# A two-layer encoder with a mixture of experts: the router works by pairs of token tiles, and the first expert's rows come from one-hot products

## What is computed

```python
def hier_moe(h, w_group, b_group, w_er, b_er, w_gate, w_up, w_down):
    ...
    g_sel = jnp.argmax(g_logit, axis=-1)             # one of 4 groups
    ...
    top_v, top_i = lax.top_k(e_logit, MOE_TOP_K)     # two of its 8 experts
    gate = jax.nn.softmax(top_v, axis=-1) * p_g[:, None]
    ...
    def expert_block(args):
        xb, e = args
        return (jax.nn.silu(xb @ w_gate[e]) * (xb @ w_up[e])) @ w_down[e]
```

## Time and profile before

| | |
|---|---|
| median of 3 runs | 1590.0 us (1588.47 to 1594.48) |
| profiled execution | 1584.55 us |
| span in its profile | 1582.7 us |
| PE busy | 1388.3 us (88%) |
| DVE busy | 529.7 us (33%) |
| moved by DMA | 479.23 MB |

### The profile page before, as it was taken

One profiled execution on the slowest core, in us unless ns is written; L12 is line 12 of the kernel. 1 busy time (PEld: TensorE's weight loads), 2 busy tenths in 40 slices (PEclk: granted clock), 3 DMA queues, 4 the chain that ended last, 5 costly groups with the idle time before them and its releaser, 6 DMA issues. The chain is left out here.

```text
span 1582.7 us, 18640 instructions
## 1 busy us (share of the span) xinstructions
PE 1388.3 (88%) x6901; PEld 640.5 (40%) x6901; DVE 529.7 (33%) x1248; ACT 244.0 (15%) x522; POOL 194.4 (12%) x362
## 2 busy tenths in 40 slices
PE   7999999999988888887889978899997887888786
PEld 4544574553333332332334456455332332333232
DVE  6999985251110111111141159335111111011115
ACT  3211121120000000000020047212100000000002
POOL 5200000011111111111000000001121111111100
PEclk9999999999999999999999989999999999999999
DMA  8314436279999999999995100537999999999996
GB/s 251 119 58 94 56 121 266 93 287 385 402 426 427 427 426 427 426 427 426 427 367 194 54 1 2 213 123 302 369 419 427 426 426 426 428 426 428 425 429 257
DMA packets 74021, 479.23 MB, mean 303 GB/s; under 512 B 16152, under 2 KB 23064, under 8 KB 49392
## 3 DMA queue, kind: packets, MB, share of 16 engines
q1 hardware_dynamic: 61392, 454.36, 71.1%
q0 software_dynamic: 11152, 19.27, 3.4%
q10 hardware_dynamic: 1424, 4.89, 0.8%
HBM read 468.01 MB, written 26.74 MB: 313 GB/s over the span
## 5 line engine op out<-in xcount | busy, mean ns | idle before, releaser
L700 PE MATMUL psum<-ring,work 128*64 128x512 f32 x992 | 475.1, 635 | 89.2 <-DMA ring<-in_moe_w_up 89.2
L701 PE MATMUL psum<-ring,work 128*64 128x512 f32 x992 | 475.7, 636 | 0.0
L700 PEld LDWEIGHTS psum<-ring,work 128*64 128x64 f32 x992 | 140.1, 146 | 397.5 <-issue 310.5
L713 PE MATMUL psum<-ring,work 128*64 128x512 f32 x992 | 226.5, 598 | 40.1 <-DVE work L886 39.8
L883 DVE TENSOR_TENSOR work<-work,psum 64x512 f32<-64x512 f32 x64 | 44.2, 690 | 557.4 <-ACT work L840 557.3
L840 ACT ACTIVATE work<-psum 64x512 f32<-64x512 f32 x64 | 37.8, 590 | 800.0 <-PE psum L701 800.0
L701 PEld LDWEIGHTS psum<-ring,work 128*64 128x64 f32 x992 | 140.2, 146 | 2.0
L713 PEld LDWEIGHTS psum<-ring,work 128*64 128x64 f32 x992 | 67.3, 136 | 157.5 <-issue 132.6
L889 DVE COPY work<-psum 128x512 f32<-128x512 f32 x60 | 41.4, 691 | 231.5 <-PE psum L713 231.5
L1793 PE MATMUL psum<-ring,hT 128*128 128x512 f32 x256 | 113.5, 600 | 0.0
L1086 POOL DMA_INDIRECT work<-h_dram,ints x64 | 66.8, 1043 | 56.9 <-POOL ints L1079 53.1
(11 more groups left out here) (382 smaller groups left out, 1406.9 us busy)
## 6 DMA issues: line engine op xcount, KB each, us to landing
ring<-in_moe_w_gate SPq DMA_DIRECT2D x62, 2048.0 KB, 16.9
ring<-in_moe_w_up SPq DMA_DIRECT2D x62, 2048.0 KB, 21.5
ring<-in_moe_w_down SPq DMA_DIRECT2D x62, 2048.0 KB, 21.9
ring<-in_hyb_w_in SPq DMA_DIRECT2D x5, 2048.0 KB, 8.9
work<-y_dram SPq DMA_DIRECT2D x8, 1024.0 KB, 9.4
ring<-in_swa_w_qkv SPq DMA_DIRECT2D x3, 2048.0 KB, 17.8
x_sb<-in_x SPq DMA_DIRECT2D x8, 512.0 KB, 6.3
y_dram<-x_sb SPq DMA_DIRECT2D x1, 4096.0 KB, 18.5
```

Source lines behind the costliest of these rows:

```text
L700: nc.tensor.matmul(bank[2 + b][0:BLK, :], x, g[:, c, :], start=c == 0, stop=c == KC - 1)
L701: i = nc.tensor.matmul(bank[2 + b][BLK:P, :], x, u[:, c, :], start=c == 0, stop=c == KC - 1)
L713: i = nc.tensor.matmul(bank[6 + b][BLK * hf:BLK * (hf + 1), :], HTE[b][:, c, :], d[:, c, hf * HALF:(hf + 1) * HALF], start=c == 0, stop=c ...
```

## The change

The router works on tiles 0 and 1 first and on tiles 2 and 3 later, each pair with logits in a bank of its own (7 and 4), a chain `groups(b)`, `experts(b)`, `places(b)` and counts of its own. The logits of tile 2 are computed as soon as its halves are out of PSUM. ACT copies both halves of the last tile; DVE evacuates a tile ahead of norming the next, and ACT takes the root behind its copy. The gather of the first expert's rows, its 4 transposes and their copy are gone. In their place DVE makes for each tile a one-hot of 64 columns (`OH0`), and `pe_x_first` multiplies `hN` by it: 16 matmuls of 64 columns for each pair. ACT copies the first pair's result (`XF`) and DVE adds the second's. The lists serve from the second expert on, and the products for target rows stand behind the first expert's gate and up products (`pe_targets`). The fillers shrink: before there are, in columns, 2 x 512 ahead of the logits of tile 2, 256 ahead of the last logits, 7 x 512 behind them, 2 x 512 and 256 behind the counts, and 3 x 512, 256 and 512 around `pe_x` of the first expert; what is left is 256 ahead of the last logits, 2 x 512 behind the first count and 256 behind the last. The load to `W2[2]` now waits for the logits only; that to `W2[1]`, which lies over `hN`, waits for the last product that reads `hN` and stands behind it.

```diff
+        def act_norm_evac_last(act, A_, n):
+
+            act.wait_ge(n_hp.s, 8 * n + 2 * NT)
+            A_(nc.scalar.copy(hT[:, 4:8, (NT - 1) * P:NT * P],
+                              bank[norm_bank(n, NT - 1) + 1][:, :].rearrange("p (c n) -> p c n", c=4)), n_ea)
...
+        OH0 = cut(WK, 9216, NT * BLK)
+        PL2 = cut(WK, 9472, 8 * BLK)
+        XF = XT[0].rearrange("p c (g n) -> p c g n", g=2)
+
+        AS = [rt("AS")[:, 3 * NE * b:3 * NE * (b + 1)] for b in range(2)]
...
-            pe.wait_ge(n_ea.s, NT * (2 * l + 1) + t + 1)
-            pe.wait_ge(n_ed.s, NT * (2 * l + 1) + t + 1)
+            pe.wait_ge(n_ea.s, act_evacs(2 * l + 1, t))
             if t == 0:
                 pe.wait_ge(g_wr.s, l + 1)
             wr = rt("wr").rearrange("p (c n) -> p c n", c=KC)
             for c in range(KC):
-                i = nc.tensor.matmul(bank[7][:, 36 * t:36 * t + 36], hT[:, c, t * P:(t + 1) * P], wr[:, c, :],
+                if c == KC // 2 and t < NT - 1:
+                    pe.wait_ge(n_ed.s, dve_evacs(2 * l + 1, t))
+                elif c == KC // 2:
+                    pe.wait_ge(n_ea.s, act_evacs(2 * l + 1, t) + 1)
+                i = nc.tensor.matmul(bank[LGB[t // 2]][:, 36 * (t % 2):36 * (t % 2) + 36], hT[:, c, t * P:(t + 1) * P], wr[:, c, :],
                                      start=c == 0, stop=c == KC - 1)
-            if t == NT - 1:
+            if t % 2:
                 i.then_inc(g_lg.s, 1)
 
+        def pe_x_first(pe, b, done):
+
+            for c in range(KC):
+                for t in range(2 * b, 2 * b + 2):
+                    i = nc.tensor.matmul(bank[4 * b][:, BLK * c:BLK * (c + 1)], hN[:, t, HALF * (c // 4) + c % 4:HALF * (c // 4 + 1):4],
+                                         OH0[:, BLK * t:BLK * (t + 1)], start=t % 2 == 0, stop=t % 2 == 1)
+            i.then_inc(done, 1)
+
         def pe_router(pe, l):
 
-            pe.wait_ge(g_A.s, l + 1)
+            s0, s1 = (AS[b][:, NE:2 * NE] for b in range(2))
+            pe.wait_ge(g_A.s, 2 * l + 1)
             pe.wait_ge(g_zero.s, 1)
-            nc.tensor.matmul(bank[1][:, 0:NE], cst("before"), rt("S"), start=True, stop=True).then_inc(g_C.s, 1)
-            nc.tensor.matmul(bank[3][:, 0:NE], ONES[:, :], rt("S"), start=True, stop=True).then_inc(g_C.s, 1)
-            pe_keep_busy(6, 512, 512, 256)
-
-            pe.wait_ge(g_exr.s, 4 * l + 3)
-            pe.wait_ge(g_L.s, l + 1)
-            pl, bl, bs = shp(PL1, 8, BLK), shp(BLT, 8, NE), shp(BLS, 8, NE)
+            nc.tensor.matmul(bank[1][:, 0:NE], cst("before"), s0, start=True, stop=True).then_inc(g_C.s, 1)
+            pe_keep_busy(6, 512, 512)
+            pe.wait_ge(g_L.s, 5 * l + 2)
+            pe_x_first(pe, 0, g_C.s)
+            pe.wait_ge(g_A.s, 2 * l + 2)
+            nc.tensor.matmul(bank[3][:, 0:NE], ONES[:, :], s0, start=True, stop=False)
+            nc.tensor.matmul(bank[3][:, 0:NE], cst("before"), s1, start=False, stop=True).then_inc(g_C.s, 1)
+            nc.tensor.matmul(bank[1][:, 2 * NE:3 * NE], ONES[:, :], s0, start=True, stop=False)
+            nc.tensor.matmul(bank[1][:, 2 * NE:3 * NE], ONES[:, :], s1, start=False, stop=True).then_inc(g_C.s, 1)
+            pe_keep_busy(6, 256)
+            pe.wait_ge(g_L.s, 5 * l + 4)
+            pe_x_first(pe, 1, e_xt)
+
+            pe.wait_ge(g_exr.s, 5 * l + 4)
+            pe.wait_ge(g_L.s, 5 * l + 5)
+            pl, bl = shp(PL1, 8, BLK), shp(BLT, 8, NE)
             for a in range(8):
                 for hf in range(2):
-                    i = nc.tensor.matmul(bank[2][BLK * hf:BLK * (hf + 1), 0:NE], pl[:, a, :], bl[:, a, :], start=a == 0,
+                    i = nc.tensor.matmul(bank[7][BLK * hf:BLK * (hf + 1), 256:256 + NE], pl[:, a, :], bl[:, a, :], start=a == 0,
                                          stop=a == 7)
             i.then_inc(g_Lm.s, 1)
-            pe.wait_ge(g_exr.s, 4 * l + 4)
+
+        def pe_targets(pe, l):
+
+            pl, bs = shp(PL1, 8, BLK), shp(BLS, 8, NE)
+            pe.wait_ge(g_exr.s, 5 * l + 5)
             for hf in range(2):
                 for a in range(8):
                     i = nc.tensor.matmul(bank[5][BLK * hf:BLK * (hf + 1), 0:NE], pl[:, a, :], bs[:, a, :], start=a == 0,
...
-            act.wait_ge(g_A.s, l + 1)
+            act.wait_ge(g_C.s, 4 * l + 2)
+            A_(nc.scalar.copy(XF, bank[0][:, :].rearrange("p (g c n) -> p c g n", g=2, c=4)), g_exr)
+            act.wait_ge(g_A.s, 2 * l + 2)
...
+            def groups(b):
+                ts = slice(2 * b, 2 * b + 2)
+                lg = rt("lg").rearrange("p (t n) -> p t n", t=NT)[:, ts]
+                dve.wait_ge(g_lg.s, 2 * l + b + 1)
+                V(tv.tensor_tensor(lg, bank[LGB[b]][:, 0:72].rearrange("p (t n) -> p t n", t=2),
+                                   ins_dim(rt("bias"), 1, 2), ALU.add))
+                V.sync()
+                gl = lg[:, :, 0:NGRP]
+                og = of_tiles("og", b).rearrange("p (t g) -> p t g", t=2)
+                first_max(V, og, gl, cst("gtie"), of_tiles("gm", b), rt("tmp")[:, 0:8].rearrange("p (t g) -> p t g", t=2))
+                V(tv.tensor_tensor(eg[:, ts], gl, ins_dim(of_tiles("gm", b), 2, NGRP), ALU.subtract), g_ex if b else None)
+
+            def experts(b):
+                ts = slice(2 * b, 2 * b + 2)
+                el = rt("lg").rearrange("p (t n) -> p t n", t=NT)[:, ts, NGRP:36]
+                og = of_tiles("og", b).rearrange("p (t g) -> p t g", t=2)
+                tmp = rt("tmp")[:, 64 * b:64 * b + 64]
+                V(tv.tensor_tensor(tmp.rearrange("p (t g e) -> p t g e", t=2, g=NGRP),
+                                   bass.AP(el.tensor, el.offset, [list(el.ap[0]), list(el.ap[1]), [EPG, NGRP], [1, EPG]]),
+                                   ins_dim(og, 3, EPG), ALU.mult))
+                V.sync()
+                es, es2 = (of_tiles(n, b).rearrange("p (t e) -> p t e", t=2) for n in ("es", "es2"))
+                V(tv.tensor_reduce(es, tmp.rearrange("p (t g e) -> p t e g", t=2, g=NGRP), AX.X, ALU.add))
+                V.sync()
+                oh = rt("oh").rearrange("p (k t e) -> p k t e", k=2, t=NT)[:, :, ts]
+                t8 = tmp[:, 0:16].rearrange("p (t e) -> p t e", t=2)
+                first_max(V, oh[:, 0], es, cst("etie"), of_tiles("v1", b), t8)
+                V(tv.scalar_tensor_tensor(es2, oh[:, 0], -3e38, es, ALU.mult, ALU.add))
+                V.sync()
+                first_max(V, oh[:, 1], es2, cst("etie"), of_tiles("v2", b), t8)
+                if b:
+                    V(tv.tensor_tensor(rt("dd"), rt("v2"), rt("v1"), ALU.subtract), g_ex)
+                Ev = rt("E").rearrange("p (k t g e) -> p k t g e", k=2, t=NT, g=NGRP)[:, :, ts]
+                for k in range(2):
+                    V(tv.tensor_tensor(Ev[:, k], ins_dim(og, 3, EPG), ins_dim(oh[:, k], 2, NGRP), ALU.mult))
+                V.sync()
+                E4 = rt("E").rearrange("p (k t e) -> p k t e", k=2, t=NT)[:, :, ts]
+                V(tv.tensor_tensor(AS[b].rearrange("p (a e) -> p a e", a=3)[:, 0::2], E4[:, 0], E4[:, 1], ALU.add))
+                V.sync()
+                V(tv.tensor_tensor(AS[b][:, NE:2 * NE], AS[b][:, 0:NE], AS[b][:, 2 * NE:3 * NE], ALU.add), g_A)
+
+            def places(b):
+                dve.wait_ge(g_C.s, 4 * l + 2 * b + 1)
+                V(tv.tensor_tensor(w3[:, 2 * b:2 * b + 2], shp(AS[b][:, 0:2 * NE], 2, NE), ins_dim(bank[1 + 2 * b][:, 0:NE], 1, 2),
+                                   ALU.add))
+                V.sync()
+                for t in range(2):
+                    V(tv.tensor_scalar(OH0[:, BLK * (2 * b + t):BLK * (2 * b + t + 1)], rt("place1"), w3[:, 2 * b + t, 0:1],
+                                       AS[b][:, 2 * NE * t:2 * NE * t + 1], ALU.is_equal, ALU.mult), g_L)
+
+            groups(0)
+            V.sync()
+            experts(0)
+            V.sync()
+            groups(1)
+            V.sync()
+            places(0)
+            experts(1)
+            V.sync()
+            places(1)
...
+            dve.wait_ge(e_xt, NE * l + 1)
+            dve.wait_ge(g_exr.s, 5 * l + 3)
+            tv.tensor_tensor(XF, XF, bank[4][:, :].rearrange("p (g c n) -> p c g n", g=2, c=4), ALU.add).then_inc(e_xe, 1)
+
             cnt = rt("C")[:, 0:NE]
-            dve.wait_ge(g_C.s, 2 * l + 2)
-            V(tv.tensor_copy(cnt, bank[3][:, 0:NE]))
-            dve.wait_ge(g_exr.s, 4 * l + 2)
+            dve.wait_ge(g_C.s, 4 * l + 4)
+            V(tv.tensor_copy(cnt, bank[1][:, 2 * NE:3 * NE]))
+            dve.wait_ge(g_exr.s, 5 * l + 2)
             V(tv.tensor_reduce(rt("pg"), eg, AX.X, ALU.add))
             V(tv.tensor_scalar_add(rt("dd"), rt("ee"), 1.0))
             dve.wait_ge(g_Lm.s, l + 1)
-            V(tv.tensor_scalar(SLL[:, 0:NE], bank[2][:, 0:NE], cst("half"), 2.0 * NOROW, ALU.add, ALU.add), g_sl)
-            V.sync()
...
+            dve.wait_ge(g_exr.s, 5 * l + 5)
             dve_late_operands(dve, V)
             dve.wait_ge(g_Om.s, 2 * l + 1)
```

(38 more changed lines are left out.)

73 lines of the change are left out of this document (26 added, 47 removed).

## The result

The changed kernel took **1601.9 us** (median of 5 runs, 1600.4 to 1602.2) against 1590.0 (1587.8 to 1594.5): ratio 1.0076, 95% interval 1.0063 to 1.0089, so slower by 12 us. The forecast was 1584.5 with a range from 1578 to 1591: wrong, in sign too. The page, against the earlier trace rows: the span is 15.9 us longer, and the line of the one-hot products, L470, now stands in the chain.

The account below looks back on a forecast made before the run. Bound by the two mixtures of experts, each paced by PE, then DMA. Step 0 starts 5.4 us earlier, step 1 2.7; 2 x 2.7 = 5.4 off the median 1590.0 gives 1584.5 us, range 1578 to 1591.

Parts of the forecast that it names:

- The end of the mixer: Norm and evacuations before the router: DVE done at 1068.5, last logits end at about 1072.3 instead of 1074.8.
- The router's chain on DVE: Groups, experts and places of both pairs: from 1068.5 to 1079.9, at 0.28 us per 64-wide instruction.
- The step that failed: One-hot products on PE (`pe_x_first`): 32 entries a pair at 0.11 each, 3.5 us, upper bound 4.5 us.
- Hidden by experts(1): First pair's one-hot products on PE, 1076.1 to 1079.6, lie under DVE's experts(1), which ends at 1079.9.
- Rival 3: Router with fewer fillers: PE idles behind the last logits, clock falls to half; 3.8 us a layer lost, 1597.5; chance 7%.
- 8.2 + 1: Half clock in the router: one-hot and list products cost 8.2 us more, the start of step 0's gate products another 1.
- PE would be busy 17 of 20 us: Router, 1066 to 1086 us: PE counted busy for some 17 of 20 us, as evidence against a falling clock.
- What is given back: Between first and second expert: uncovered target products 1.6 us and gather stall 1.1; gain falls from 5.4 to 2.7 a layer.
- The gather: Second expert's rows: issued at 1087.7, lands 6.4 us later at 1094.1, PE waits 1.1 us.
- That the end moves with PE: SP issues loads when PE has used a slot, so DMA backlog and end follow PE: 2 x 2.7 = 5.4 us.

Follow-up runs that it names:

- x8: Kernel before with only the change's end of the mixer (norm, waits, order of evacuations), its router and fillers kept: 1583.7 us.
- x10: Changed kernel with packed one-hot weight loads (output not the reference's) and three 512-column fillers around the last two tiles' logits: 1582.2 us.
- x1: Changed kernel with nine 512-column fillers per layer put back ahead of and behind the last logits: 1615.8 us.
- x6: Changed kernel with packed one-hot weight loads (output not the reference's) and the nine 512-column fillers put back around the last logits: 1596.2 us.
- x5: Changed kernel with one-hot weight loads from 128 columns side by side, no fillers put back (output not the reference's): 1589.8 us.
- x4: Changed kernel with one-hot as stationary operand, hN streaming 512 wide, rows copied and transposed, target products ahead of step 0 again: 1581.1 us.
- x11: x4 run a second time, unchanged, with no more fillers: 1581.0 us.
- x2: Kernel before with only the fillers that the change removes taken out (14 of 512 columns, 2 of 256 per layer): 1602.4 us.
- x7: x4 with eight more fillers in its router: around the logits, behind the first pair's products and around the transposes: 1582.7 us.
- x9: x4 with four more 512-column fillers: one ahead of tile 2's logits, one behind the last, two behind the first pair's products: 1581.3 us.

## Why the prediction was wrong, point by point

- **The end of the mixer** held: DVE began at 1076.64, forecast 1076.8, and x8 shows the part by itself as a gain, of 4.8 us by the medians.
- **The router's chain on DVE** held: experts(1) ended at 1087.88 against 1088.2; a 64-wide instruction lasted 0.22 to 0.23 and stood 0.26 from start to start (x10), for my 0.28.
- **The step that failed: "The nearest row is L1529, 8 entries in 1.06 us ... 0.11 each, so 3.5 us", upper bound 4.5.** The one-hot products took 7.5, at full clock too (x1). L1529 was near in shape and not in how the stationary operand lies: its is packed. With packed operands the same 32 entries took 3.68 (x6, x10), so the number was right for another program. L345, the upper bound, does take the very slices of `pe_x_first`, but as transposes, which this stride costs little (0.14 us each). So the bounds came from a packed product and a strided transpose, and no row was a strided product; the range could not hold the truth. "Hidden by experts(1)" fell with it: with strided operands the first pair outlasts its cover by 3.8.
- **Rival 3, "the clock falls", 7%,** came about and was underpriced in chance: without the fillers it fell for 18 us or more in both layers of the change and in one of x5, and for some 3 to 10 us in x5's other layer and in x4 and x11. The price of the products and the gate products was about right: 8.2 + 1 forecast, 9.6 measured (x5). The sum was too low: it left out the 1.6 us of target products and whatever else runs slow ahead of step 1. It has step 1 come 3.8 us later, and in x5's layer 0, packed with the clock down, it comes 7.6 later. The mechanism was half right: the gap behind the last logits was to bring the fall, and in layer 1 it came ahead of that gap, with PE busy. What spoke against it, that PE would be busy 17 of 20 us, proved no protection. The Trainium skill's rule in "TensorE: Matmul & The Clock Gate", section on why this matters, that idle gaps between bursts bring half rate, is borne out by x2 (2.36 us idle in layer 0 before the fall); it doesn't cover x1 or layer 1 of the change, where no gap came before the fall.
- **What is given back** was near, 1.9 us for the forecast's 2.7: in x10 the last up product of step 0 to the first of step 1 takes 1.9 us more than before (1097.83 to 1101.41 there, 1091.38 to 1096.88 here); 1.6 of it are the targets, 0.4 the gather.
- **The gather** landed 5.7 us after its issue (x10), forecast 6.4; the wait was 0.42. In the change it was no wait, since step 0 itself ran slow. The Trainium skill's rule in "DMA: Bandwidth & Descriptors", section on queues, rings and completion order, that DMA engines take turns between queues, would have had it after 4.0 us by the prediction's own working; the row lies between the two.
- **That the end moves with PE** held: in the change step 1 comes 8.5 and 7.1 us later, 15.6 in sum, and the span is 15.9 longer. In x10 it comes 3.6 us earlier in each layer (forecast 2.7) and the median is 7 lower. Over all twelve kernels the shifts of step 1 in the two layers add up to that of the median within some 4 us.
- With both faults repaired (x10) it takes 1582.2, near the 1584.5 that stood in the forecast: the plan was right, and its price was of operands that the kernel doesn't have and of a clock that its fillers didn't keep.

What stays open: what brings the clock down while PE is busy. It did so in narrow logits and in strided products. x6, the same as x1 but for the stride, kept it, so in that place the stride decides, but by what it does to the array no run here tells. Also open is what decides between two layers of one program (x5), and why strided slices load fast in a transpose. The clock is read from one profile of each kernel.

## What to carry to other kernels

Before a matmul is priced from a row, compare how its stationary operand lies and whether the row is a product or a transpose, not its shape alone: at full clock a stride of four 32-bit columns made the load 329 ns instead of 192 and doubled every narrow product, while a transpose of the same columns took 0.14 us. If the order of columns is free, or the wide operand can be the moving one, take that (x4: 1.94 us for 7.5). Fillers are part of a schedule's price: whoever removes a wait that they covered puts a few back where PE would stand, and none where they outlast the wait (x7, x9). By the sorting above one belongs between long rows of narrow products too, though PE has no gap there.

## What the runs showed of the hardware

- A 128x128 f32 weight load of a product took 192 ns from columns side by side and 329 from every fourth at 1.00 (x6, x1); at 0.50 it took 333 and 330 (x5, x1). Loads of the same strided columns for a transpose took 211 at the median and 231 at most (the change). The spacing of strided products was the same at both clock levels (7.50 us a pair in x1's layer 0 at 1.00, 7.52 to 7.73 in the change at 0.50), that of packed ones was not (3.68 and 6.93).
- The clock fell to 0.50 in x1 though PE was busy 16.00 of 16.00 us before, in strided products, and in layer 1 of the change though it was busy from 1040 to 1076, in logits of 36 columns.
- A router whose PE ran at half clock cost 9.6 us a layer, and taking nothing but fillers out of the kernel before cost 13 us in all.
